# Laying woven pieces by an estimated load into the gaps between weighted sums, and one head of queries to a gap

## What is computed

```
mod = silu(c) @ w_ada + b_ada                       # shift1, scale1, gate1, shift2, scale2, gate2
h   = rmsnorm(x) * (1 + scale1) + shift1
q, k, v, B, C, hc = split(h @ w_in)                 # 2304 columns
zB  = window attention (8 heads, 2 KV heads, window 128, ALiBi, sinks)
zA  = B * causal conv of width 3 (C * hc)
x   = x + gate1 * (concat[zB, zA] @ w_out)
h2  = rmsnorm(x) * (1 + scale2) + shift2
# PEER: 8 heads, 128 x 128 product keys, top 16 of 16384 experts for each token and head
q   = h2 @ wq ; scores against both halves of the keys ; top 16 of each half ; top 16 of the 256 sums
act = gelu(u_tab[experts] . h2) ; y = sum(softmax(best) * act * v_tab[experts])
x   = x + gate2 * y ; rmsnorm
```

## Time and profile before

| | us |
|---|---|
| median of the runs | 3530.96 |
| span of the profiled execution | 3240.6 |
| what lies around the span (difference to the median) | 290.4 |
| PE busy | 1805.4 |
| DVE busy | 2039.2 |
| ACT busy | 704.0 |
| POOL busy | 2065.3 |

### The profile page before, as it was taken

The page is one execution under the profiler, slowest core; times in us unless marked ns, Lnnn a source line. Parts: engine busy times, 40 slices in busy tenths (PEclk is TensorE's granted clock), DMA queues, the critical chain, the costliest instruction groups (busy, mean ns, idle before and its releaser), DMA issues.

```text
span 3240.6 us, 31526 instructions
## 1 busy us (share of the span) xinstructions
PE 1805.4 (56%) x9968; PEld 839.9 (26%) x9968; DVE 2039.2 (63%) x5142; ACT 704.0 (22%) x1968; POOL 2065.3 (64%) x2211
## 2 busy tenths in 40 slices
PE   5988578786567832464444444444444444454443
PEld 2446364443222310131211211221111121122200
DVE  3334835667787775557666766666666666666663
ACT  2121212221332221122222112222222222211211
POOL 1232646666575575657777777777777677777774
PEclk8999789897768966676677667776667767666667
DMA  8835999999999899989999999999999999999997
GB/s 308 266 105 197 377 378 376 410 409 401 384 393 404 349 411 404 410 344 410 409 409 409 409 409 406 408 404 407 402 408 404 404 409 402 405 408 403 404 406 301
DMA packets 393188, 1228.50 MB, mean 379 GB/s; under 512 B 54563, under 2 KB 104719, under 8 KB 389678
## 3 DMA queue, kind: packets, MB, share of 16 engines
q0 software_dynamic: 305728, 1109.92, 86.6%
q1 hardware_dynamic: 46314, 75.12, 6.5%
q10 hardware_dynamic: 40980, 41.44, 3.9%
HBM read 1211.31 MB, written 16.04 MB: 379 GB/s over the span
## 4 chain that ended last, share of the span: by engine, by line
POOL 28%; DMA 26%; DVE 15%; PE 14%; issue 11%; DVEq 2%; ACT 1%; ACTq 1%; SPq 1%; POOLq 0%
DMA arena<-in_peer_u,eid 20%; POOL arena L481 14%; POOL arena L492 14%; DVE arena L1531 9%; DMA arena<-in_peer_v,eid 4%; PE PS L687 3%; PE PS L816 2%; PE PS L649 2%; PE PS L632 2%; PE PS L661 1%; DVE arena L1520 1%; PE PS L737 1%; ACTq L935 1%; PE PS L699 1%; DVE arena L1515 1%
## 5 line engine op out<-in xcount | busy, mean ns | idle before, releaser
L1531 DVE CUSTOM_DVE_ANT_0 arena<-arena,PS 128x1024 f32<-128x1024 f32 x1056 | 1244.7, 1216 | 787.9 <-DMA arena<-in_peer_u,eid 605.8
L816 PE MATMUL PS<-arena 128*32 128x512 f32 x4224 | 816.9, 913 | 1174.1 <-DMA arena<-in_peer_v,eid 1164.3
L481 POOL DMA_INDIRECT arena<-in_peer_u,eid x1056 | 1000.0, 947 | 481.9 <-issue 292.2
L492 POOL DMA_INDIRECT arena<-in_peer_v,eid x1040 | 986.8, 949 | 489.9 <-issue 288.8
L816 PEld LDWEIGHTS PS<-arena 128*32 128x32 f32 x4224 | 163.8, 144 | 1632.8 <-issue 1619.6
L1143 ACT ACTIVATE arena<-sel,wgt 128x32 f32<-128x32 f32 x1056 | 230.8, 310 | 26.7 <-DVE wgt L1542 22.9
L649 PE MATMUL PS<-arena 128*128 128x256 f32 (+1 forms) x576 | 172.1, 454 | 21.8 <-DVE arena L1374 17.5
L786 PEld LDWEIGHTS PS<-arena 128*128 128x128 f32 x1280 | 152.6, 199 | 45.7 <-issue 41.0
L1131 ACT ACTIVATE arena<-PS 128x256 f32<-128x256 f32 x42 | 16.1, 384 | 677.4 <-PE PS L797 677.4
L786 PE MATMUL PS<-arena 128*128 128x128 f32 x1280 | 160.2, 285 | 3.3 <-ACT arena L1126 3.3
L1126 ACT ACTIVATE arena<-PS 128x256 f32<-128x256 f32 (+1 forms) x48 | 17.2, 358 | 598.5 <-PE PS L786 598.5
(11 more groups left out here) (241 smaller groups left out, 1942.3 us busy)
## 6 DMA issues: line engine op xcount, KB each, us to landing
arena<-in_w_ada SPq DMA_DIRECT2D x24, 1024.0 KB, 8.7
arena<-in_peer_u,eid POOLq DMA_INDIRECT x1056, 10.4
arena<-in_peer_v,eid POOLq DMA_INDIRECT x1056, 7.8
arena<-in_peer_wq ACTq DMA_DIRECT2D x10, 1024.0 KB, 5.5
arena<-in_peer_wq SPq DMA_DIRECT2D x4, 2048.0 KB, 40.9
arena<-in_w_in SPq DMA_DIRECT2D x14, 512.0 KB, 8.6
arena<-in_w_in ACTq DMA_DIRECT2D x14, 512.0 KB, 15.9
arena<-in_x_prompt ACTq DMA_DIRECT2D x8, 512.0 KB, 9.0
```

Source lines behind the costliest of these rows:

```text
L481: po.indirect_dma_start(out=Ur[:, k % RING, :], out_offset=None, in_=a["peer_u"], in_offset=bass.IndirectOffsetOnAxis(ap=eid[m % 4][:, k:k ...
L492: po.indirect_dma_start(out=Vr[:, k % RING, :], out_offset=None, in_=a["peer_v"], in_offset=bass.IndirectOffsetOnAxis(ap=eid[m % 4][:, k:k ...
L816: last = mm(PS[j * GT:(j + 1) * GT, half, :], dsel[m % 2][:, k, :], rows[:, k % RING, half * 512:(half + 1) * 512], start=m % 2 == 0 and q ...
L1531: last = ve.tensor_tensor_reduce(out=Ur[:, k % RING, :], in0=Ur[:, k % RING, :], in1=hP, scale=1.0, scalar=0.0, op0=ALU.mult, op1=ALU.add, ...
```

## The change

A function gaps() lays the pieces out instead of a fixed rate. Each kind has an estimated load (LOAD; an I piece 8 or 5 by its half). A gap takes its first piece whatever its load, and further ones while the sum is at most FIT = 9 and the count at most MOST, which is 1, 3, 2 and 1 for the four gaps. All three engines read the same table. The pieces now begin in turn 1 and end in turn 20. On DVE the second and third piece of the second gap are answered in one place, behind b = 4. Tile 3's queries stand one head to a gap in turns 22 and 23, ahead of the weighted sum; head 0 of tile 4 stands in the last gap of turn 23. The load of the bias moves from UT 1 to the fourth gap of turn 12 (I 33), ahead of the outputs and w_out.

```diff
-RATE = 6
+LOAD = {"T": 2, "X": 2, "Q": 7, "W": 2, "VN": 1, "KN": 1, "UT": 1, "S": 2, "P": 2, "V": 2, "H0": 7, "H1": 7}
+FIT, MOST = 9, (1, 3, 2, 1)
+def gaps():
+    out, i = [[[], [], [], []]], WB
+    while i < len(PIECES):
+        step = [[], [], [], []]
+        for gap, most in zip(step, MOST):
+            load = 0
+            while i < len(PIECES) and len(gap) < most:
+                kind, n = PIECES[i]
+                load += 8 - 3 * (n % 2) if kind == "I" else LOAD[kind]
+                if gap and load > FIT:
+                    break
+                gap.append(i)
+                i += 1
+        out.append(step)
+    return out
...
@@ PE
-                if i < last_i:
-                    piece(i)
-                if 1 <= n <= UNITS:
-                    weigh(n - 1, 0)
...
+                for q in range(NV):
+                    for i in gap(n, q)[:1]:
+                        piece(i)
+                    if q == 1 and n % 2 == 1 and n >= 3:
+                        combine((n - 3) // 2)
+                    for i in gap(n, q)[1:]:
+                        piece(i)
+                    if n in (FIRST - 2, FIRST - 1):
+                        queries(AHEAD, HU * (n - FIRST + 2) + q)
+                    if q == NV - 1 and FIRST <= n + 2 < UNITS:
+                        scores(n + 2)
+                    if q == NV - 1 and n == FIRST - 1 or q == 1 and n >= FIRST and t < TT:
+                        queries(t, h)
+                    if 1 <= n <= UNITS:
+                        weigh(n - 1, q)
@@ ACT
-                        ac.dma_start(biasP, a["alibi_p"]).then_inc(s["biasB_ld"], 16)
...
+                if kind == "I" and n == 2 * len(ORDER) - 3:
+                    ac.dma_start(biasP, a["alibi_p"]).then_inc(s["biasB_ld"], 16)
...
-                for q in range(RATE - 1):
-                    if i + q < last_i:
-                        piece(i + q)
+                for i in after_weight:
+                    piece(i)
+                for q in range(NV - 1):
+                    for i in gap(n, q):
+                        piece(i)
...
@@ DVE
-                after = {2: i, 3: i + 1, 4: i + 2, 5: i + 3, 6: i + 4}
+                after = {2: gap(n, 0), 3: gap(n, 1)[:1], 4: gap(n, 1)[1:], 5: gap(n, 2)[:1], 6: gap(n, 2)[1:], 0: gap(n - 1, 3)}
```

More of the change, by code:

```diff
@@ L1166, in _ @@
                     gelu(n - 1)
-                left = n >= 2 and i - 1 < last_i
-                after_weight = left and PIECES[i - 1][0] in ("S", "H1", "KN", "VN", "UT")
-                if left and not after_weight:
-                    piece(i - 1)
+                left = gap(n - 1, NV - 1)
+                after_weight = [i for i in left if PIECES[i][0] in ("S", "H1", "KN", "VN", "UT")]
+                for i in left:
+                    if i not in after_weight:
+                        piece(i)
                 if n % 2 == 1 and n + 1 < UNITS:
@@ L1184, in _ @@
                         take_queries(AHEAD, h2)
-                if n >= FIRST - 1 and t < TT:
+                if n >= FIRST and t < TT:
                     take_queries(t, h)
@@ L1586, in _ @@
                             first_norm(2)
-                        if b == 0 and n >= 2 and i - 1 < last_i:
-                            piece(i - 1)
-                        if b in after and after[b] < last_i:
-                            piece(after[b])
+                        for i in after.get(b, ()):
+                            piece(i)
                         if f is not None and b == 5:
```

38 lines of the change are left out of this document (6 added, 32 removed).

## The result

The changed kernel takes 3512.07 us (median, 3505.30 to 3515.86), the kernel before beside it 3531.16 us (3530.26 to 3542.48): 19.1 us or 0.8% faster, ratio 0.9917 [0.9894, 0.9941]. The forecast was 3521 with a range of 3500 to 3543, "faster" at 0.56.

What follows compares the result with a forecast made beforehand. The prediction took the 66 turns as bound by bytes at about 410 GB/s; its terms summed to -10 us on the 3240.6 us span, giving 3230.6, plus 290.4 us taken to lie around the program: 3521 us, range 3500 to 3543.

Steps and rivals of the forecast that it cites:

- The cap of 36 us: Turns up to 27: most that moving pieces could win, from time when the DMA engines had nothing to do.
- Queries: Tile 3's queries, one head to a gap instead of four and five together: -9 us, bounds -13 and -5.
- Q, W and ACT's loads: Turns 1 to 4: third sum done before ACT's w_in issue stalls, -9 us; earlier pairs of Q, -1.
- Turn 1: Three X pieces and Q 0 come ahead of sums that had less ahead of them: +1 us.
- I pieces: Four to a turn instead of six, where transfers are already full, so nothing to win: 0.
- the rival of the low clock: I turns: PE stays at the low clock, nine turns, +27 us, total 3548; chance 0.06.
- Attention: S, P and V pieces in turns 14 to 16: DVE needs 45.0 us against 41.84; +5 us, bounds -3 and +12.
- the rival "slower": Pieces sharing seven gaps in turns 14 to 16, 18 and 19 hold back the weighted sum: 3545; chance 0.13.
- same place: Attention turns of the kernel before, where the prediction read 3.3 us of lost transfers.
- Tail: H0, H1 and T pieces shifted by a gap, T 3 and H0 5 sharing one: +2 us, bounds -8 and +12.
- wq: Load of wq waits for the last piece, issued about 45 us later: +1 us, bounds 0 and +6.
- Bias load: Moved ahead of w_out's loads to turn 12, where the slow stretch is full of transfers: 0, bounds -2 and 0.

Runs made afterwards that it cites:

- e1_before: The kernel before, unchanged, profiled again on a chip at the fast rate: 3247.22 us, ratio 1.0002.
- e11_before: The kernel before, unchanged, run for its trace at the fast rate: 3242.52 us, span 3240.7.
- e14_before: The kernel before, unchanged, run for its trace on another chip at the slow rate: 3531.60 us (one run), span 3529.8.
- e3_queries_only: The kernel before with only tile 3's queries laid one head to a gap: 3233.55 us, ratio 0.9956, at the fast rate.
- e4_gaps_only: The changed kernel with tile 3's queries back in the second gap, four and five heads together: 3255.36 us, ratio 1.0030, at the fast rate.
- e12_pairs_loads: The changed kernel with at most two pieces a gap, I pieces at load 4, and ACT's w_in loads in three parts: 3494.80 us, ratio 0.9909, slow rate.
- e2_after: The changed kernel, unchanged, run again on a chip at the fast rate: 3245.53 us, ratio 0.9999.
- e8_pairs_two: The changed kernel with at most two pieces in any gap and every I piece at load 4: 3232.01 us, ratio 0.9951, at the fast rate.
- e13_slots: The changed kernel with the second gap's third piece answered later on DVE, PE's order untouched: 3490.07 us, ratio 0.9921, at the slow rate.

## Why the prediction came out as it did

**The base failed.** "290.4 us ... lies around the program and stays": false. e1_before, e11_before and e14_before have under 2 us around their spans. The 290 us are spread over the turns (46.5 for 41.84 us), in which the transfers of the timed executions are slower. The cap of 36 us and every hole were read at a rate that the timed runs didn't have, and 3521 is 3531 less a sum made for another rate. At the rate that it was made for, -10 is to be compared with -0.1. That 3521 lies near 3512 is luck: no term of the sum was made for the rate at which this was measured. (A slip without weight: the deepest of the slices that it reads is not 344 GB/s but the last one, at 301.)

**Queries, -9 (bounds -13 to -5): right, somewhat small.** e3_queries_only has -12.1, the windows 14.8 to 0.3 us; taken off the changed kernel (e4_gaps_only) the term is 9.8 us. At the slow rate the profiles say more: turns 22 to 27 take 305.9 us in the one profile of before and 270 to 286 in the four of kernels with one head to a gap (276.2 in the changed kernel). The same four heads that hold a gap for 16.8 us in the earlier trace rows hold it for 31.7 us in e14_before:

```profile
1436.55 3.98 PE L786 MATMUL PS<-arena 128*128 128x128 f32 x32
1454.50 5.18 PE L786 MATMUL PS<-arena 128*128 128x128 f32 x32 [13.98 <-ACT arena L1126]
```

The second head waits 14 us for ACT. By the kernel ACT waits there for PE's first head alone, which was done at 1440.5, and it comes at 1454.07; the profile names no cause, and that stays open. POOL stands 19.7 us twice there; at the fast rate its longest wait is 10.2 us. In the changed kernel at the slow rate the longest in turns 22 to 26 is 5.9 us, but its profile has no such stall of ACT. e12_pairs_loads, also with one head to a gap, has two, each holding PE 14.3 us; POOL then stands up to 12.1 us, and turns 23 and 24 run at 315 GB/s. So one head to a gap does not hide such a stall; how much of the 29.7 us is the layout and how much the stall is not shown.

**Q, W and ACT's loads, -9 and -1: right in kind, half the size.** Turns 2 to 4 give -5.3 at the fast rate. The hole after Q 7, which the -9 was to fill, gave 3 of them; the rest came with the Q pieces. Turn 4 of e1_before and of e2_after:

```profile
473.00:536.20 63.20, 47.11 (x373) 28.97 (x374) 27.21 (x74) 15.87 (x34) 31.95 (x34) 0.81 0.91 334
```

```profile
475.80:535.80 60.00, 28.00 (x296) 16.35 (x296) 27.04 (x74) 14.12 (x30) 29.83 (x33) 0.73 0.95 351
```

That is 11.7 and 8.6 us starved. PE's idle time ahead of W 1 stayed, as forecast, and is longer than the 20.5 us of the earlier trace rows (e2_after, W L669, the sum L844):

```profile
469.25 1.97 PE L844 MATMUL PS<-arena 128*32 128x512 f32 x16
498.31 3.65 PE L669 MATMUL PS<-arena 128*32 128x128 f32 x64 [27.09 <-ACT arena L1025]
```

But "no window under 350 GB/s beside it" was wrong. Two windows of e2_after beside it:

```profile
486.00:498.00 12.00, 0.00 (x0) 0.00 (x0) 0.00 (x0) 0.77 (x1) 0.00 (x0) 0.50 1.01 352
498.00:510.00 12.00, 11.19 (x209) 8.00 (x213) 5.43 (x14) 8.87 (x24) 4.69 (x5) 0.84 0.69 199
```

The third sum was done ahead of the stall and its rows kept the engines full for some 12 us more, then they were spent. The step that failed is "the issue itself is not changed": the six loads took ACT 30.4 us and not 24.7, so the hold had grown, from 20.5 to 27 us, with the reserve. Why their issue took longer is not tested. At the slow rate the six loads take ACT 6.9 us in the changed kernel and 9.2 in e14_before, and turns 1 to 4 came out 18.2 us shorter (214.2 for 232.4) in that one pair; more than all of it is turn 3 (55.4 for 76.0 us). PE stands some 20 us in turns 2 to 4 of both on "issue", where e2_after has 2.1, so the fast rate's account of these turns can't be carried over.

**Turn 1, +1: measured +5.6.** Three X pieces in its second gap; the prediction saw them and put next to nothing on them. With two there, e8_pairs_two is back at 4.3 us starved, so the cost is that of the triple, with Q 0 behind it.

**I pieces, 0: right.** Turns 6 to 9 of e2_after run at 410 GB/s:

```profile
559.00:735.00 176.00, 124.34 (x527) 61.42 (x528) 109.86 (x284) 36.09 (x103) 118.98 (x126) 0.86 1.04 410
```

The granted clock is 0.86, between the two levels and nearer the high one; the rival of the low clock, and with it the rule of the Trainium skill, "TensorE: Matmul & The Clock Gate", section "HAM oscillation — how this bites in real kernels" (keep matmuls contiguous), decided nothing here. The clock did stand at 0.50 in the 12 us in which PE had no work (the window at 486 above), and cost nothing that shows.

**Attention, +5 (bounds -3 to +12): failed in size, measured +15.8.** This is the step that was mis-sized. It was summed as DVE's time: 45.0 us a turn for 41.84. DVE was 40.14 us busy of 46.40 in turn 15:

```profile
1007.00:1053.40 46.40, 26.61 (x128) 11.17 (x124) 40.14 (x96) 18.35 (x58) 32.68 (x34) 0.74 0.99 383
```

It had 6 us to spare, and in turns 13 to 16 it waited 27.1 us for rows of u that POOL had asked for late. The stall of the second part behind S is there (4.5 us in two) and is small. What counts is the hold of the second sum, and the rival "slower" had that mechanism, though not turn 13 and turn 1 among its places: from sum to sum it is 22.1, 21.6, 19.9 and 22.0 us in turns 13 to 16 of e2_after, so some 18 us of hold once the sum itself is taken off. By the rival's price, what goes beyond 12.6 us, that is 4 x 5.4 = 22 us, and 25.4 were starved (8.9, 7.0, 3.1 and 6.3 by turn, so the price holds for the sum and not for each). Turn 18's 29.1 us stand where before had a hole as large; by the price they cost some 13 us, and 7.3 were starved. The rival's mechanism and, roughly, its price were right; the queries and turns 2 to 4 gave as much back, so it ended at no change. The "same place" that lost 3.3 us before was also taken too small: turns 10 to 14 of e1_before have 9.6.

**Tail, +2 (bounds -8 to +12): measured -4.9.** One hole was left, in turn 18, as forecast. **wq, +1: 0.** In the first profile of the changed kernel it was issued from 1348.87 to 1371.15 and the queries at 1428.30 didn't wait. **Bias load, 0:** not measured apart. In e2_after it is issued at 894.82, as turn 12 ends (409 GB/s); the slow stretch at a full DMA share stands behind the loads of w_out, as before.

At the fast rate the terms are then -14.5, -5.3, +5.6, +15.8, -4.9 and 0 = -3.3 for a measured -0.1. Two signs that the prediction named for being wrong came: a hole near 10 us after Q 7, and DVE under 41 us in turn 15, though with transfers that were not full. At the slow rate one pair of profiles gives -18 over turns 1 to 4, +18 over 5 to 21, -32 over 22 to 26 and +11 after that. So the layout of the pieces is a loss at the fast rate, by e4_gaps_only, and the queries are a gain. At the slow rate, that of the result, this pair points the same way, with the layout near nothing and the queries as the gain, but no run there has the one without the other.

## What to carry to other kernels

Compare the span of a profile with the time of its own run before anything else; here a span 8% under the median of the runs was another rate, not time around the program, and sums made on it hold for that rate alone. Where short jobs answer each other through other engines, pack them by the answers waited for, not by their work: two such jobs ahead of a step that frees a buffer cost 11 us starved where three cost 25, and one each, with that step between, had the lowest time at the tail, by a margin within the intervals. Even work that is all needed at once (four heads of 4.2 us) was better laid one to a gap, by 12 us.

## What the runs showed of the hardware

- The same program runs at two transfer rates, steady turns of 41.8 us (405 GB/s) on one chip and 46 to 46.5 us (364 to 366) on another: 3246 and 3523 us. The median packet is the same; 2.5% against 0.4% take over 300 ns, which makes the mean 5% longer (172 for 164 ns) where the turn is 11% longer. PE has 130.3 us of waits without a shown cause in turns 30 to 60 of e14_before and none in e1_before.
- The changed kernel's ratio depends on the rate: 0.9999 [0.9989, 1.0008] at the one, 0.9917 [0.9894, 0.9941] at the other; e13_slots, which differs from it on DVE alone, has 0.9921 [0.9891, 0.9950] at the slow one.
- Issuing six loads on ACT's queue took 24.7 us in the first profile and 30 in e2_after (466.83 to 497.18) at the fast rate, and 6.9 and 9.2 us at the slow one; two of them alone took 17.6 us.
